# A hybrid decoder layer on eight cores: the last supertile's residual kept on chip, its silu inputs parked in SBUF, and a new order of early loads and of GpSimd's turns

## The chip, the cores and the metric

The kernel runs on the 8 NeuronCores of one Trainium2 chip. Each core takes one of the 8 sequences of the batch and shares nothing with the others but the weights that it reads. The metric is the device time of the slowest core, in microseconds. A core has TensorE (PE, matrix products into PSUM), VectorE (DVE), ScalarE (ACT), GpSimd (POOL, which cannot read PSUM) and SyncE (SP, which here only issues DMAs). PSUM has 8 banks of 128 x 512 floats.

## The reference, cut to what matters

```python
h = rmsnorm(x, norm_g)                                  # x: (8, 4096, 1024)
q, k, v, z_a, u_s, v_s, z_s = split(h @ w_in + b_in)    # 512,128,128,512,512,512,512 columns
attn = banded_sink_attention(q, k, v, sinks) * silu(z_a)
sgu = gelu(u_s) * (W_s @ layernorm(gelu(v_s)) + b_s) * silu(z_s)
x = x + concat(attn, sgu) @ w_out + b_out
out = rmsnorm(x, final_norm_g)
```

Attention has 8 query heads of 64 over 2 key heads, a window of 128 keys, and is evaluated on blocks of 128 queries against their own and the previous block of keys. W_s is a lower-triangular 128 x 128 matrix per group of 64 channels, applied inside chunks of 128 positions.

## The kernel before, in words

A core's 4096 rows are 32 tiles of 128 rows, four to a supertile of 512 (NS = 8 supertiles, `st`). Weights are loaded once, scaled by the norm's gain and kept in bf16 (`w_fm`, `w_vs`, `w_v`, line 463); w_out comes in bf16 through eight DMAs on GpSimd's queue (`load_w_out`, line 777).

For a supertile, x is loaded into `xa` (line 429, four slots, one per tile), squared on ScalarE (468), its norm finished in two small GpSimd steps (474, 477), scaled into `xn` (482, 483) and transposed into `xT`: through PSUM for the first two supertiles, by a DMA transpose (493) later. `fm_group` (511 to 528) makes 128 output columns for 512 rows: eight matmuls of 128 x 128 by 512 (line 517) into a bank, and an eviction with the bias: on ScalarE or VectorE for q and k (523, 524), on ScalarE with gelu or silu for u, z_s, z_a (527). `qkv` also makes v (542, 546). `vs_tile` (571 to 589) makes v_s with its layer norm, `mix_part` (617 to 629) the spatial gating. `attention` (645 to 704) handles one block: scores (647), exponential (652), mask multiply (665 on VectorE, 660 on GpSimd), sum of the two halves (682), values and denominators (674, 677), log and exponential of the denominator (690, 694), gate (696), and the product into `mixT` (701).

The output of a tile: `load_xe` loads the same rows of x again, as the residual, into one of four slots of `xe` (709), and GpSimd adds b_out to it (711). `out_tile` does two halves of eight matmuls (725), each evicted by VectorE into xe (730), a square on ScalarE (733), two GpSimd steps (735, 737), a scaling on VectorE by the norm and gain (739), and the store (742). A slot of xe is loaded again once its store has landed. The four loads of the last supertile are issued from the end of `build_program`'s loop (816 to 818).

The order of the work is not written by hand. `Graph.op` records every operation with what it reads and writes, a planned cost in us, and a priority (lower goes first); `Scheduler.run` then plays the program through with these costs and gives each engine a fixed order, always taking the operation that can start earliest. Three of its rules matter here. ScalarE works in phases, because each of its functions needs its own table: gelu, silu and exp of a supertile follow each other, with a table load between (line 424 in the trace), and matmul groups for gelu and silu have a gate: they are not planned before their phase, or the end of the one before it. PSUM banks have classes with a cap each (line 111): S for scores, pairs of banks; V for values and denominators, two per block; P for everything else. And operations marked `port=True` on VectorE and GpSimd are planned so as not to overlap (lines 141 to 143, 222). On the chip only semaphores hold: `emit` (268) gives each operation waits for its `deps`, and planned times that don't come true are not kept. Each engine, and each queue of DMA issues on SP, works strictly in its order.

```python
            if o.port and e in ("dve", "pool"):
                port[0] = free[e]
```

## Time and profile before

| what | value |
|---|---|
| median of 3 runs | 534.2 us (534.0 to 534.81) |
| the profiled execution, its own time | 536.34 us |
| its span, slowest core (core 0) | 534.8 us |
| spans of the eight cores | 528.0 to 534.8 us |
| TensorE busy | 483.6 us |
| VectorE busy | 379.2 us |
| ScalarE busy | 325.6 us |
| GpSimd busy | 191.6 us |

The profile is one execution on the slowest core; its times run from the first instruction. Busy times count instructions at work, not waits. An instruction that is held up inside, by a shared resource, shows as a long one. In a window or page row, the clock is the share of TensorE's full clock that was granted.

### The profile page before, as it was taken

How to read it: one execution, taken by the hardware profiler on the slowest of the kernel's cores; microseconds unless marked ns; L12 is line 12 of the kernel's file. 1: busy time of each engine (PE TensorE's matmuls, PEld its weight loads, DVE VectorE, ACT ScalarE, POOL GpSimd, SP SyncE). 2: the span in 40 equal slices, each digit the busy share in tenths (PEclk: the TensorE clock that was granted, in tenths of full speed). 3: DMA queues.
4: the chain of work that ended last, by engine and by line, in shares of the span. 5: the costliest groups of instructions: out<-in, count | busy, mean ns of one | idle time of the engine just before them, and what ended most of it. 6: DMA issues, size and time to landing. Idle time of an engine off the chain costs nothing.

```text
span 534.8 us, 9042 instructions; the slowest of 8 cores (528.0 to 534.8 us)
## 1 busy us (share of the span) xinstructions
PE 483.6 (90%) x2802; PEld 221.5 (41%) x2852; DVE 379.2 (71%) x527; ACT 325.6 (61%) x565; POOL 191.6 (36%) x232
## 2 busy tenths in 40 slices
PE   1799986898999999999999999999999999999960
PEld 0357442344444434444444434443444435443320
DVE  1676889659778767778775597766757687557963
ACT  4363393855677475847675756858578575348621
POOL 1030564125023331333236254542364215450444
PEclk9999997999999999999999999999999999999985
DMA  7999993593008801336532933356342213300363
GB/s 233 329 344 324 313 232 50 106 253 116 1 40 203 230 1 40 120 66 172 159 104 59 210 101 119 119 94 146 126 152 65 51 63 136 119 1 39 120 182 132
DMA packets 44543, 73.12 MB, mean 137 GB/s; under 512 B 27600, under 2 KB 27728, under 8 KB 44496
## 3 DMA queue, kind: packets, MB, share of 16 engines
q1 hardware_dynamic: 43200, 70.40, 44.5%
q0 software_dynamic: 1152, 2.10, 2.4%
q8 instruction: 23, 0.38, 0.3%
q14 instruction: 24, 0.20, 0.1%
q10 hardware_dynamic: 144, 0.05, 0.1%
HBM read 51.56 MB, written 16.78 MB: 128 GB/s over the span
## 4 chain that ended last, share of the span: by engine, by line
PE 79%; issue 5%; DVE 4%; ACT 4%; POOL 3%; DMA 3%; SPq 0%; POOLq 0%; DVEq 0%; ACTq 0%
PE pp L517 40%; PE pp L725 18%; PE pp L571 9%; PE pp L674 3%; PE pp L647 3%; PE pp L542 2%; DMA xa<-x 2%; PE pp L556 1%; DMA xe<-x 1%; PE pp L677 1%; PE pp L617 1%; DVE PT L665 1%; DVE xe L739 1%; POOL w_out_bf L777 1%; ACT PT L652 1%
## 5 line engine op out<-in xcount | busy, mean ns | idle before, releaser
L517 PE MATMUL pp<-xT,w_fm 128*128 128x512 bf16 x1056 | 243.0, 382 | 6.9 <-DVE sgt L625 1.6
L517 PEld LDWEIGHTS pp<-xT,w_fm 128*128 128x128 bf16 x1088 | 104.2, 98 | 134.8 <-issue 15.9
L725 PE MATMUL pp<-w_out_bf,mixT 128*128 128x512 bf16 x497 | 117.8, 384 | 6.2 <-DVE mixT L701 3.8
L711 POOL TENSOR_TENSOR xe<-xe,bout_sb 128x1024 f32<-128x1024 f32 x32 | 77.4, 2423 | 29.7 <-DMA xe<-x 29.6
L725 PEld LDWEIGHTS pp<-w_out_bf,mixT 128*128 128x128 bf16 x512 | 47.9, 99 | 69.1 <-issue 18.0
L733 ACT ACTIVATE junk<-xe 128x1024 bf16<-128x1024 f32 x32 | 34.0, 1062 | 53.8 <-DVE xe L730 48.5
L730 DVE TENSOR_TENSOR xe<-pp,xe 128x512 f32<-128x512 f32 x64 | 43.4, 685 | 28.9 <-PE pp L725 24.1
L652 ACT ACTIVATE PT<-pp 128x1024 bf16<-128x1024 f32 x63 | 62.6, 1030 | 0.9 <-PE pp L647 0.9
L571 PE MATMUL pp<-w_vs,xT 128*128 128x512 bf16 x221 | 53.7, 391 | 6.6 <-DVE v_r L546 5.3
L739 DVE SCALAR_TENSOR_TENSOR xe<-xe,st_fr,gf_sb 128x1024 f32<-128x1024 f32 x32 | 47.1, 1473 | 15.4 <-POOL st_fr L737 9.5
L665 DVE TENSOR_TENSOR PT<-PT,pack_b_sb 128x1024 bf16<-128x1024 bf16 x57 | 50.4, 898 | 4.8 <-ACT PT L652 4.0
L690 ACT ACTIVATE LR<-pp,esink 128x128 f32<-128x128 f32 x128 | 36.3, 365 | 26.7 <-PE pp L677 26.0
L578 ACT ACTIVATE vs_f<-vs_f 128x512 f32<-128x512 f32 x32 | 19.6, 627 | 42.0 <-DVE vs_f L576 40.5
L735 POOL TENSOR_SCALAR st_fm<-st_fs 128x1 f32<-128x1 f32 x32 | 9.9, 309 | 95.9 <-ACT junk L733 95.4
L527 ACT ACTIVATE zaT<-pp,pack_a_sb 128x512 bf16<-128x512 f32 x32 | 21.7, 691 | 33.5 <-PE pp L517 32.2
L576 DVE TENSOR_TENSOR vs_f<-pp,bvs_sb 128x512 f32<-128x512 f32 x32 | 22.0, 688 | 26.1 <-PE pp L571 21.9
L468 ACT ACTIVATE junk<-xa 128x1024 bf16<-128x1024 f32 x32 | 33.7, 1055 | 6.0 <-DMA xa<-x 5.2
L571 PEld LDWEIGHTS pp<-w_vs,xT 128*128 128x128 bf16 x224 | 21.8, 100 | 35.5 <-issue 11.9
L629 POOL TENSOR_TENSOR mixT<-sgt,uT 128x512 bf16<-128x512 f32 x19 | 22.0, 1156 | 40.6 <-DVE sgt L625 33.8
L625 DVE SCALAR_TENSOR_TENSOR sgt<-pp,pack_b_sb,Cmat 128x512 f32<-128x512 f32 x32 | 23.2, 745 | 16.5 <-PE pp L617 8.9
L584 POOL TENSOR_SCALAR st_ve<-st_mv 128x1 f32<-128x1 f32 x32 | 8.5, 266 | 71.0 <-DVE st_mv L582 70.1
L424 ACT ACT_TABLE_LOAD x24 | 30.8, 1283 | 1.9 <-POOL ones L439 1.5
(63 smaller groups left out, 542.6 us busy)
## 6 DMA issues: line engine op xcount, KB each, us to landing
xa<-x SPq DMA_DIRECT2D x32, 512.0 KB, 8.4
xe<-x SPq DMA_DIRECT2D x32, 512.0 KB, 4.1
out<-xe SPq DMA_DIRECT2D x32, 512.0 KB, 2.9
xe<-w_in SPq DMA_DIRECT2D x12, 512.0 KB, 12.1
mixT<-w_in SPq DMA_DIRECT2D x10, 512.0 KB, 14.3
w_out_bf<-w_out POOLq DMA_DIRECT2D x8, 256.0 KB, 15.7
LR<-sgu_wT SPq DMA_DIRECT2D x1, 512.0 KB, 11.4
bout_sb<-bout_bc SPq DMA_DIRECT2D x1, 512.0 KB, 13.1
```

The source lines that it names most:

```text
L424: return lambda e: e.activation(out=dmy[:, 1:2], in_=dmy[:, 0:1], func=func)
L468: G.op("act", lambda e: e.activation(out=junk[:], in_=xa[:, tt, :], func=AF.Square, accum_out=st_ss[:, par, tt:tt + 1]), reads=[("xa", tt) ...
L517: ins = e.matmul(bank(h), lhsT=w_fm[:, FM.index(cb), k, :], rhs=xT[:, xb, k, :], start=(k == 0), stop=(k == 7))
L571: ins = e.matmul(bank(h), lhsT=xT[:, xb, k, tt * 128:(tt + 1) * 128], rhs=w_vs[:, k, :], start=(k == 0), stop=(k == 7))
L652: G.op("act", lambda e, h=h, kb=kb: e.activation(out=PT[:, p2, kb, :], in_=bank2(h), func=AF.Exp, scale=0.125), uses=[h], writes=[("PT", p ...
L665: return e.tensor_tensor(out=v, in0=v, in1=mask[kb].unsqueeze(1).to_broadcast([128, 8, 128]), op=ALU.mult)
L690: ins = e.activation(out=LR[:, lb, c * 128:(c + 1) * 128], in_=bank(hd)[:, c * 128:(c + 1) * 128], func=AF.Ln, bias=esink[:, c:c + 1])
L711: G.op("pool", lambda e: e.tensor_tensor(out=xe[:, s, :], in0=xe[:, s, :], in1=bout[:], op=ALU.add), reads=["c_bout"], writes=[("xe", s, 0 ...
L725: ins = e.matmul(bank(h), lhsT=mixT[:, mb, ec, tt * 128:(tt + 1) * 128], rhs=w_out[:, ec, hf * 512:(hf + 1) * 512], start=(ec == 0), stop= ...
L730: G.op("dve", lambda e, hf=hf, h=h: e.tensor_tensor(out=xe[:, s, hf * 512:(hf + 1) * 512], in0=bank(h), in1=xe[:, s, hf * 512:(hf + 1) * 5 ...
L733: G.op("act", lambda e: e.activation(out=junk[:], in_=xe[:, s, :], func=AF.Square, accum_out=st_fs[:, s:s + 1]), reads=[("xe", s, 0), ("xe ...
L739: G.op("dve", lambda e: e.scalar_tensor_tensor(out=xe[:, s, :], in0=xe[:, s, :], scalar=st_fr[:, s:s + 1], in1=gf[:], op0=ALU.mult, op1=AL ...
```

## The change

There are five parts. (1) The last supertile's output uses `xa`, which still holds its x, in place of xe: `load_xe` is not called for it, b_out is added to xa by GpSimd, and the result is stored from xa; for the others nothing is changed but that the addition now stands in `out_tile`. (2) The last supertile's eight silu matmul groups have no gate; their result plus bias is copied to SBUF in fp32, by VectorE or ScalarE, into the other buffer of xT (z_s) and the weights of q (z_a), after the last readers of these; ScalarE applies silu from there in the silu phase. (3) The loads of the third supertile's x, of the first supertile's residual and of the final gain wait until the last part of w_out has landed, and w_out's operations are recorded earlier. (4) A GpSimd operation marked for the port waits for the VectorE operation marked for it that the plan has just before; line 739 is marked too. The other way round there is no wait. (5) Class V may hold three banks. Beside these, matmuls that write column ranges of one bank set the start flag only on the bank's first matmul; `full` and `onto` of a bank are new and `onto` is used by no caller. The diff, cut to its core:

```diff
...
+        for r in behind:
+            deps[id(r)] = r
...
-    CAPS = {"S": 4, "V": 2, "P": 4}
+    CAPS = {"S": 4, "V": 3, "P": 4}
...
-        port = [0.0]
+        port = [0.0, None]
...
             if o.port and e in ("dve", "pool"):
-                port[0] = free[e]
+                if e == "pool" and port[1] is not None and port[1].eng == "dve" and port[1] not in o.deps:
+                    o.deps.append(port[1])
+                port[:] = [free[e], o]
...
         def load_xa(st, tt):
             after = [w_op[X1_AFTER[tt] - 1]] if st == 1 else [w_op[NCB - 1]] if st == 2 else ()
             o = G.op("sp", lambda e: e.dma_start(out=xa[:, tt, :], in_=x_d[(4 * st + tt) * 128:(4 * st + tt + 1) * 128, :]),
-                 writes=[("xa", tt)], cost=0.5, dsem=d_xa[tt], kb=512, prio=st - 1.5 + 0.01 * tt, after=after)
+                 reads=[("w_out", 7)] if st == 2 else [], writes=[("xa", tt)], cost=0.5, dsem=d_xa[tt], kb=512, prio=st - 1.5 + 0.01 * tt, after=after)
...
-            G.op("pe", mm, reads=[("xT", xb, t) for t in range(4)] + [("w", cb)], cost=1.73, alloc=[h], prio=prio, mode="full", gate=ph)
+            pre = st == NS - 1 and func == AF.Silu
+            G.op("pe", mm, reads=[("xT", xb, t) for t in range(4)] + [("w", cb)], cost=1.73, alloc=[h], prio=prio, mode="full",
+                 gate=None if pre else ph)
...
+            if pre:
+
+                i = cb - CB_ZS
+                if i < 4:
+                    mem, old = xT[:, 1 - xb, 2 * i:2 * i + 2, :].rearrange("p a b -> p (a b)"), [("xT", 1 - xb, t) for t in range(4)]
+                else:
+                    mem, old = w_fm[:, i - 4, :, :].rearrange("p a b -> p (a b)"), [("w", CB_Q + i - 4)]
+                mem = mem.bitcast(F32)
+                G.op({"dve": (0.745, lambda e: e.tensor_scalar(out=mem, in0=bank(h), scalar1=bias, scalar2=None, op0=ALU.add)),
+                      "act": (0.69, lambda e: e.activation(out=mem, in_=bank(h), func=AF.Identity, bias=bias))},
+                     None, uses=[h], reads=["c_biasfm"], writes=[("pre", i)], prio=prio, behind=[r for k in old for r in G.rd[k]])
+                G.op("act", lambda e: e.activation(out=dst, in_=mem, func=func), reads=[("pre", i)], writes=[key], cost=0.6,
+                     prio=prio - 0.3, phase=ph)
+            elif func is None:
...
-                                       rhs=w_v[:, k, :], start=(k == 0), stop=(k == 7))
+                                       rhs=w_v[:, k, :], start=(k == 0 and tt == 0), stop=(k == 7),
+                                       skip_group_check=True)
...
-            G.op("sp", lambda e: e.dma_start(out=xe[:, s, :], in_=x_d[n * 128:(n + 1) * 128, :]), writes=[("xe", s, 0), ("xe", s, 1)],
+            G.op("sp", lambda e: e.dma_start(out=xe[:, s, :], in_=x_d[n * 128:(n + 1) * 128, :]), writes=[("xe", s), ("xe", s, 0), ("xe", s, 1)],
+                 reads=[("w_out", 7)] if st == 0 else [],
                  cost=0.5, dsem=d_xe[s], kb=512, prio=st + 0.2 + 0.1 * s)
-            G.op("pool", lambda e: e.tensor_tensor(out=xe[:, s, :], in0=xe[:, s, :], in1=bout[:], op=ALU.add),
-                 reads=["c_bout"], writes=[("xe", s, 0), ("xe", s, 1)], cost=2.6, prio=st + 0.6 + 0.1 * s, port=True)
...
+            last = st == NS - 1
+
+            buf, key = (xa, ("xa", s)) if last else (xe, ("xe", s))
+            G.op("pool", lambda e: e.tensor_tensor(out=buf[:, s, :], in0=buf[:, s, :], in1=bout[:], op=ALU.add),
+                 reads=["c_bout"], writes=[key], cost=2.4, prio=st + 0.6 + 0.1 * s, port=True)
...
-                def mmo(e, hf=hf, h=h):
+                cols = slice(hf * 512, (hf + 1) * 512)
+                need = [("mixA", mb, tt)] + [("mixS", mb, jj) for jj in range(4)] + [("w_out", k) for k in range(8)]
+                def mmo(e, cols=cols, h=h):
...
-                G.op("pe", mmo, reads=[("mixA", mb, tt)] + [("mixS", mb, jj) for jj in range(4)] + [("w_out", k) for k in range(8)],
-                     cost=1.73, alloc=[h], prio=v0 + 0.05 * hf, mode="full")
-                G.op("dve", lambda e, hf=hf, h=h: e.tensor_tensor(out=xe[:, s, hf * 512:(hf + 1) * 512], in0=bank(h),
-                                                                  in1=xe[:, s, hf * 512:(hf + 1) * 512], op=ALU.add),
-                     uses=[h], writes=[("xe", s, hf)], cost=0.68, prio=v0 - 0.5)
...
+                G.op("pe", mmo, reads=need, writes=[("oT", h)], cost=1.73, alloc=[h], prio=v0 + 0.05 * hf, mode="full")
+                G.op("dve", lambda e, cols=cols, h=h: e.tensor_tensor(out=buf[:, s, cols], in0=bank(h), in1=buf[:, s, cols], op=ALU.add),
+                     uses=[h], reads=[("oT", h), key], writes=[key + (hf,)], cost=0.68, prio=v0 - 0.5)
+            both = [key + (0,), key + (1,)]
...
-            G.op("dve", lambda e: e.scalar_tensor_tensor(out=xe[:, s, :], in0=xe[:, s, :], scalar=st_fr[:, s:s + 1], in1=gf[:],
+            G.op("dve", lambda e: e.scalar_tensor_tensor(out=buf[:, s, :], in0=buf[:, s, :], scalar=st_fr[:, s:s + 1], in1=gf[:],
                                                          op0=ALU.mult, op1=ALU.mult),
-                 reads=[("fr", s), "c_gf"], writes=[("xe", s, 0), ("xe", s, 1)], cost=1.39, prio=v0)
-            G.op("sp", lambda e: e.dma_start(out=out_d[n * 128:(n + 1) * 128, :], in_=xe[:, s, :]),
-                 reads=[("xe", s, 0), ("xe", s, 1)], cost=0.5, dsem=d_xe[s], kb=512, prio=v0, final=True)
+                 reads=[("fr", s), "c_gf"], writes=both, cost=1.3, prio=v0, port=True)
+            G.op("sp", lambda e: e.dma_start(out=out_d[n * 128:(n + 1) * 128, :], in_=buf[:, s, :]),
+                 reads=both, writes=[key], cost=0.5, dsem=d_xa[s] if last else d_xe[s], kb=512, prio=v0, final=True)
...
             load_const("c_bout", bout[:], bout_d, eng="sp", kb=512, prio=-0.3, after=[w_op[21]])
-            load_const("c_gf", gf[:], gf_d, eng="sp", kb=512, prio=-0.3, after=[w_op[21]])
+            load_const("c_gf", gf[:], gf_d, eng="sp", kb=512, prio=-0.3, after=[w_op[21]], reads=[("w_out", 7)])
...
         for cb in range(NCB):
             load_w(cb)
+        load_w_out()
...
         setup_late()
-        load_w_out()
...
         for tt in range(4):
-            load_xe(4 * (NS - 1) + tt)
             out_tile(4 * (NS - 1) + tt)
...
```

## Rows read from the trace of the kernel before

**Rows 1.** The page, busy us of each engine, share of the span, instructions.

```profile
PE 483.6 (90%) x2802; PEld 221.5 (41%) x2852; DVE 379.2 (71%) x527; ACT 325.6 (61%) x565; POOL 191.6 (36%) x232
```

**Rows 2.** Windows: length; busy PE, PEld, DVE, ACT, POOL (count); clock; DMA; GB/s.

```profile
60.00:64.00 4.00, 3.95 (x25) 1.79 (x24) 3.35 (x7) 0.00 (x0) 3.85 (x5) 1.00 1.02 335
...
70.00:108.00 38.00, 29.46 (x186) 12.85 (x188) 31.92 (x39) 25.09 (x47) 15.21 (x11) 0.91 0.62 124
108.00:478.00 370.00, 363.31 (x2055) 163.57 (x2093) 265.88 (x389) 241.80 (x422) 137.35 (x159) 1.00 0.39 110
478.00:502.00 24.00, 23.79 (x117) 9.16 (x117) 18.50 (x25) 17.30 (x29) 6.29 (x8) 1.00 0.18 67
502.00:520.00 18.00, 13.93 (x60) 5.44 (x60) 14.21 (x15) 6.66 (x16) 8.31 (x11) 0.91 0.48 141
520.00:534.80 14.80, 0.00 (x0) 0.00 (x0) 5.64 (x7) 2.30 (x4) 6.15 (x6) 0.57 0.37 148
```

**Rows 3.** Timeline, 70 to 108 us: start, us, engine, line, instructions merged.

```profile
74.29 10.63 POOL L711 TENSOR_TENSOR xe<-xe,bout_sb 128x1024 f32<-128x1024 f32 x4
...
75.83 9.64 DVE L665 TENSOR_TENSOR PT<-PT,pack_b_sb 128x1024 bf16<-128x1024 bf16 x4
...
87.42 5.84 PE L571 MATMUL pp<-w_vs,xT 128*128 128x512 bf16 x16 [5.26 <-DVE v_r L546]
...
93.96 3.63 PE L725 MATMUL pp<-w_out_bf,mixT 128*128 128x512 bf16 x16
```

**Rows 4.** Lines 665 and 739, whole span: ns min/median/max, first and last start.

```profile
L665 DVE TENSOR_TENSOR PT<-PT,pack_b_sb x57: 678/684/2842, 75.8 to 500.0; 128x1024 bf16<-128x1024 bf16 x57
...
L739 DVE SCALAR_TENSOR_TENSOR xe<-xe,st_fr,gf_sb x32: 1269/1284/3165, 104.7 to 530.4; 128x1024 f32<-128x1024 f32 x32
```

**Rows 5.** Timeline, 510 us to the end.

```profile
511.01 3.16 DVE L739 SCALAR_TENSOR_TENSOR xe<-xe,st_fr,gf_sb 128x1024 f32<-128x1024 f32 x1 [0.45 <-POOL st_fr L737]
511.03 8.81 PE L725 MATMUL pp<-w_out_bf,mixT 128*128 128x512 bf16 x31 [3.01 <-DVE mixT L701]
...
514.70 1.21 SPq L709 DMA_DIRECT2D xe<-x  x2
...
521.56 4.64 POOL L711 TENSOR_TENSOR xe<-xe,bout_sb 128x1024 f32<-128x1024 f32 x2 [2.59 <-DMA xe<-x]
...
526.37 1.29 DVE L730 TENSOR_TENSOR xe<-pp,xe 128x512 f32<-128x512 f32 x2 [1.02 <-POOL xe L711]
```

**Rows 6.** Waits: engine, line, waited for: us in total, times, longest.

```profile
DVE xe L739 <- POOL st_fr L737: 9.5, 9, 2.6
...
DVE xe L730 <- POOL xe L711: 4.6, 2, 3.6
...
PE pp L674 <- DVE mixT L701: 1.4, 1, 1.4
```

**Rows 7.** Timeline of SP: DMA issues from 46 to 103 us.

```profile
46.86 4.29 SPq L429 DMA_DIRECT2D xa<-x  x4
52.06 4.93 SPq L709 DMA_DIRECT2D xe<-x  x4
98.77 4.30 SPq L493 DMA_TRANSPOSE xT<-xn  x3
```

**Rows 8.** The tile w_out_bf: its DMA issues, and us from issue to landing.

```profile
L777 POOL DMA_DIRECT2D w_out_bf<-w_out x8: 535/557/760, 60.1 to 67.5; - x8
...
DMA to landing us min/median/max: 9.0/15.7/18.2
```

**Rows 9.** The page, DMA queue 0: packets, MB, share of 16 engines.

```profile
q0 software_dynamic: 1152, 2.10, 2.4%
```

**Rows 10.** Groups by line: busy us, mean ns, idle before.

```profile
L424 ACT ACT_TABLE_LOAD x24 | 30.8, 1283 | 1.9 <-POOL ones L439 1.5
...
L578 ACT ACTIVATE vs_f<-vs_f 128x512 f32<-128x512 f32 x32 | 19.6, 627 | 42.0 <-DVE vs_f L576 40.5 <-DVE st_mv L582 1.5
...
L524 ACT ACTIVATE qT<-pp,pack_a_sb 128x512 bf16<-128x512 f32 x17 | 11.6, 692 | 17.4 <-PE pp L517 17.3
```

More of the change, by code:

```diff
@@ L44, with __init__ @@
 class Bank:
-    def __init__(self, cls, size=1):
-        self.cls, self.size = cls, size
+    def __init__(self, cls, size=1, full=True, onto=False):
+        self.cls, self.size, self.full, self.onto = cls, size, full, onto
         self.at = None
@@ L70, in op @@
     def op(self, eng, fn, reads=(), writes=(), cost=0.1, prio=0.0, alloc=(), uses=(), phase=None, gate=None, mode=None,
-           dsem=None, kb=0, final=False, after=(), port=False):
+           dsem=None, kb=0, final=False, after=(), port=False, behind=()):
         o = Op()
@@ L164, in pick_banks @@
                     if any(bank_owner[c] is not None or c in taken for c in cells):
+                        continue
+                    if b.onto and not all(bank_full[c] for c in cells):
                         continue
@@ L236, in run @@
                         bank_owner[c] = b
+                        bank_full[c] = b.full
                         for u in bank_last[c]:
@@ L415, in build_program, with load_const @@
         d_once = []
-        def load_const(key, dst, src, eng="act", kb=64, prio=0.0, after=()):
+        def load_const(key, dst, src, eng="act", kb=64, prio=0.0, after=(), reads=()):
             s = sem(f"d_c{len(d_once)}")
             d_once.append(s)
-            G.op(eng, lambda e: e.dma_start(out=dst, in_=src), writes=[key] if isinstance(key, str) else key, cost=0.5,
+            G.op(eng, lambda e: e.dma_start(out=dst, in_=src), reads=reads, writes=[key] if isinstance(key, str) else key, cost=0.5,
                  dsem=s, kb=kb, prio=prio, after=after)
@@ L495, in transpose_x @@
                 return
-            h = Bank("P")
+            h = Bank("P", full=False)
             def tr(e):
@@ L724, in mmo @@
                     for ec in range(8):
[L725 removed]
+                        ins = e.matmul(bank(h), lhsT=mixT[:, mb, ec, tt * 128:(tt + 1) * 128], rhs=w_out[:, ec, cols],
                                        start=(ec == 0), stop=(ec == 7))
                     return ins
[L728 to L729 removed]
@@ L735, in out_tile @@
+                G.op("dve", lambda e, cols=cols, h=h: e.tensor_tensor(out=buf[:, s, cols], in0=bank(h), in1=buf[:, s, cols], op=ALU.add),
+                     uses=[h], reads=[("oT", h), key], writes=[key + (hf,)], cost=0.68, prio=v0 - 0.5)
+            both = [key + (0,), key + (1,)]
+            G.op("act", lambda e: e.activation(out=junk[:], in_=buf[:, s, :], func=AF.Square, accum_out=st_fs[:, s:s + 1]),
+                 reads=both, writes=["junk", ("fs", s)], cost=1.25, prio=v0)
             G.op("pool", lambda e: e.tensor_scalar(out=st_fm[:, s:s + 1], in0=st_fs[:, s:s + 1], scalar1=1.0 / D, scalar2=EPS,
```

15 lines of the change are left out of this document (7 added, 8 removed).

## The prediction

> **What bounds the kernel now.** I read the busy shares first, then the idle time of TensorE stretch by stretch, then what ended it in the two stretches where it is large. TensorE is busy for 483.6 of 534.8 us, VectorE for 379.2 [rows 1], so the question is where TensorE's 51 us of idle time lie. By stretch [rows 2]: of 370 us between 108 and 478 it is idle for 6.7 (370 - 363.31), of 24 until 502 for 0.2, but of 38 us between 70 and 108 for 8.5 (38 - 29.46), between 502 and 520 for 4.1 (18 - 13.93), and after 520 it does nothing for 14.8. The remaining 16.9 us, before 70, are the start, where inputs and weights arrive. The middle is TensorE's. An edit is worth something at 70 to 108, in which the first supertile's attention runs, or at the end.
>
> At 70 to 108, one wait stands out [rows 3]. GpSimd adds b_out to four residual tiles without a break (10.63 us), and four of VectorE's mask multiplies (line 665) lie beside them for 9.64 us. A mask multiply alone takes 0.68 us, at worst 2.84, which is about one GpSimd add [rows 3, 4]: VectorE stands still until the add is over. TensorE then waits 5.26 us for v_r, queued behind these multiplies, and the 16 matmuls after that take 5.84 us where 16 of the same size take 3.63 soon after [rows 3]: the granted clock is 0.91 of full over the stretch [rows 2], TensorE having been idle, and these run near the lower level, 1.2 instead of 2.4 GHz.
>
> At the end, the last two residual tiles are requested at 514.70, because their slots in xe must first be scaled (3.16 us on VectorE beside a GpSimd add, 1.28 as a rule) and stored [rows 4, 5]. Their b_out additions start at 521.56, when TensorE has finished (511.03 + 8.81 = 519.84). The tail therefore waits for a load, though the same rows of x were read for the norm.
>
> **The change part by part.** Durations are of the profiled execution: span 534.8 us, its own time 536.34, so 1.5 lie around the span; the median of the runs is 534.2, 2.1 below that time. I work out what the span loses and take it from the median.
>
> *Residual kept in xa.* Four loads and their issues go; four b_out additions of 2.3 us (4.64 for two, [rows 5]) stay, but can run as soon as xa is scaled, long before the end. The tail becomes: TensorE ends, the last eviction, square, two small GpSimd steps, scaling, store. TensorE's work from 502 on is 13.93 us [rows 2]. Its last 31 recorded matmuls (32 issued) took 8.81 us [rows 5]; at 3.63 us per 16 [rows 3] they would take 7.3, so 1.5 are slow clock and 12.4 are work: TensorE could end at 514.4 instead of 519.8. From the last eviction's start (526.37 plus half of 1.29) to the span's end are 7.8 us [rows 5], and with 0.2 allowed for the semaphore ahead of it 8.0. The best end is 522.4, a gain of 12.4. But the fourth attention block's chain still ends in an output tile that nothing can hide entirely: of the 4.1 us idle I keep 2.1, and take **10.3**. The lower end is 2.7, see the third rival. VectorE, the next in line, is busy for 18.50 + 14.21 + 5.64 us from 478 on [rows 2], partly in blocked instructions, so it could be done before 520 and isn't the bound.
>
> *GpSimd waits its turn.* Every GpSimd instruction marked for the port now waits for the VectorE one that the planner put before it. What it removes at 70 to 108: the excess of the four multiplies, 9.64 - 4 x 0.68 = 6.9 us of VectorE, seen by TensorE as 5.26 us of wait and 5.84 - 3.63 = 2.2 us of slow clock. I take **7.5**. Above, the whole stretch could give 8.5 + 2.2 = 10.7; below, 0, if the stall moves to another place. Queued behind a waiting add on GpSimd are the small steps of the norms (lines 584, 587, 735, 737), and behind those VectorE's scalings; VectorE already waits 9.5 us for st_fr in all [rows 6]. Over the middle VectorE is busy 265.88 of 370 us [rows 2], so even a doubled wait is covered: cost 0, and at worst what the fifth rival says. Marking line 739 as a port user falls under the same sum.
>
> *w_out ahead of residual loads.* Now the third supertile's x (four loads issued from 46.86), the first residuals (four from 52.06) and gf go ahead of w_out on the DMA engines, and w_out's eight transfers land up to 18.2 us after issue, the last issued at 67.5 [rows 7, 8]. In the changed kernel these nine loads wait in SP's queue for w_out; behind them on SP are only the transposes of the third supertile, at 98.77 now [rows 7]. w_out takes 2.4% of the span on all engines, 12.8 us [rows 9]; issued from 60.1 [rows 8], it should have landed at about 76. The nine loads, 4.7 MB at 335 GB/s, the rate of 60 to 64 us [rows 2], take another 14, until 91 or so with landing. The first output projections run at 94 [rows 3], and GpSimd's additions get later, which by itself moves them away from these multiplies. Gain and cost 0; cover lost, the price is the second rival's.
>
> *Silu inputs of the last supertile.* The eight matmul groups lose their gate, so they can fill idle slots in earlier phases; TensorE's work is the same. Added: eight evictions of 0.69 us [rows 10], 5.5 us; the silu itself now reads SBUF, 0.63 instead of 0.69 [rows 10]. ScalarE is idle for a third of the middle and VectorE for over a quarter [rows 2], so this is hidden. What may not be: the silu phase becomes a ScalarE-only stretch of two table loads of 1.28 and 8 x 0.63 us, 7.6 us in all [rows 10], under which TensorE can only run output projections that were filler for the last attention. Value 0; ends: a gain of 2, if the attention starts earlier, and a loss of 7.6.
>
> *Third V bank.* One wait of line 674 for line 701, 1.4 us [rows 6], goes; up to 6.7 us of middle idle could [rows 2]. Below, a third V bank takes a bank from the projections: a loss of the same size. I take **1.0**, nearest the row. The start flags of matmuls add no instruction.
>
> Sum: 10.3 + 7.5 + 1.0 = 18.8 us. The span becomes 516.0, the median 534.2 - 18.8 = **515.4 us**.
>
> **The rivals.**
> *The stall is not removed.* Only GpSimd waits; a multiply that comes late still meets an add under way and loses up to 2.16 us (2.84 - 0.68). For it: the planner of before kept the two apart on paper as well. Against: the four adds run without a break now, which a wait for the multiply between them forbids. Without the 7.5: 522.9 us.
> *w_out lands late.* It is issued while VectorE is busy for 3.35 us of the 4 from 60 to 64 [rows 2], and nine loads now stand behind it. If it lands at about 85 as now (67.5 + 18.2), the residuals land from 87 to 100, and the wait for them replaces the stall: the 7.5 are gone, 522.9 us. Against: these landing times come from a queue with 4.7 MB of other loads ahead. The Trainium skill ("SBUF — State Buffer", the box on the DVE blocks DMA trap) says that a DMA issued from GpSimd's queue cannot get its descriptors written while VectorE holds the port pair; it speaks for this rival, and by it the sum would be 11.3 us instead of 18.8. The trace here shows late landing, but not whether port or queue causes it.
> *The end turns to ScalarE.* The 7.6 us stretch uses up TensorE's filler, the last attention then leaves TensorE idle that long, and the tail gains 10.3 - 7.6 = 2.7: 523.0 us. For it: the last supertile has no next one to fill with. Against: with these projections as filler TensorE was idle for only 0.2 us between 478 and 502 [rows 2], so that there is some room.
> *Nothing in sum.* The first or second of these with the third leaves 2.7 + 1.0 = 3.7 us, and bank waits of that size end at 534.2.
> *Slower.* One mechanism: the turn-taking makes the b_out additions late. Each of 32 waits for a VectorE instruction, the eviction (line 730) waits for the addition, its bank is held, and TensorE stands. It decides from 18.8 / 32 = 0.6 us per addition that reach TensorE. With the whole 1.28 us of a scaling instruction [rows 4] in two of three additions (0.85 each), 27 us: 534.2 - 18.8 + 27 = 542.4 us. Against: TensorE is idle for only 6.7 us in the middle, and VectorE waited for an addition only twice, 4.6 us in all [rows 6].
>
> **How the numbers follow.** Forecast 0.62; stall not removed 0.10; w_out late 0.08; ScalarE at the end 0.12; nothing in sum 0.02; slower 0.06. The likeliest case gives 515.4. Its best is 12.4 + 10.7 + 2 = 25.1 less than 534.2, about 509. The three middle cases end at 523; with 1.5 for bank waits the range ends at 524.5. It leaves out 0.08 and the edges of the forecast. A measurement of this kernel tells about 0.2%, 1 us. Faster 0.92, the same 0.02, slower 0.06.
>
> **What would show it.** Right: no load into xe after the seventh supertile's; no line 665 row of 2.8 us in an unbroken series near 80, and v_r not waited for; matmuls at full clock between 80 and 95; last store about 8 us after TensorE's last matmul, and TensorE's end near 508 in a span near 516. Silu evictions beside earlier phases, middle idle still about 6 us. Wrong: GpSimd additions still in a block across multiplies; the first residual landing after 87 with line 730 waiting for it; TensorE idle for over 5 us in the last attention; TensorE waiting for line 730 throughout.

## The result and the profile after

The changed kernel takes 518.06 us (median of four runs, 517.63 to 519.86) against 534.5 us of the kernel before on the same chip, a ratio of 0.970 [0.967, 0.973]. The forecast was 515.4; the gain of 16.4 us is 2.4 less than the 18.8 of the sum. The sign and the size are about right, but the runs below give the parts other prices than the prediction did. Several chips were used, so each run is given as a ratio to the kernel before on its own chip; 0.001 is 0.53 us. On the last of these chips one half ran at a lower granted clock in most runs, so for three kernels only cores 4 to 7, the undisturbed half, are compared with the same cores of the kernel before.

The page of the changed kernel, slowest core (own time 518.4, span 516.8), with busy time by engine and the group of VectorE's mask multiply:

```profile
PE 486.8 (94%) x2852; PEld 220.7 (43%) x2852; DVE 355.9 (69%) x524; ACT 339.6 (66%) x576; POOL 180.7 (35%) x232
...
L694 DVE TENSOR_TENSOR PT<-PT,pack_b_sb 128x1024 bf16<-128x1024 bf16 x58 | 42.9, 760 | 1.8 <-ACT PT L681 1.5
```

The mask multiplies take 42.9 us for 58, where 58 of 0.68 are 39.4. Before it was 50.4 for 57, on the page of that kernel, so 8 of some 12 us of standing still are gone; the longest single one still takes 2.83 us, about as in [rows 4]. By stretch, in the columns of [rows 2]:

```profile
70.00:108.00 38.00, 34.16 (x206) 14.60 (x205) 25.67 (x39) 24.89 (x48) 15.99 (x13) 0.91 0.63 163
108.00:478.00 370.00, 369.78 (x2109) 164.02 (x2106) 255.42 (x389) 260.50 (x439) 141.34 (x164) 1.00 0.40 114
478.00:502.00 24.00, 24.00 (x123) 9.34 (x122) 21.75 (x33) 18.15 (x37) 2.62 (x6) 1.00 0.11 44
502.00:520.00 18.00, 6.02 (x28) 2.55 (x26) 9.73 (x11) 4.24 (x8) 3.71 (x10) 0.82 0.43 175
```

TensorE's idle time between 70 and 108 fell from 8.5 us to 3.8 on this core, still at a mean clock of 0.91 (on all eight, from 6.4 to 8.5 us to 1.1 to 4.1). After 502 it works for 6 us instead of 13.9. In the middle it fell from 6.7 us to 0.2, but most of that is no gain. The trace of before on this core has 2802 matmuls [rows 1], the changed one 2852: 50 records are missing, 32 of line 517, 15 of line 725, 3 of line 571. Core 1 of before, which has no gaps, shows:

```profile
108.00:478.00 370.00, 368.30 (x2101) 164.28 (x2100) 264.21 (x390) 242.80 (x425) 138.44 (x160) 1.00 0.39 112
```

The middle had 1.7 us to give there, and 1.7 to 3.6 on the six cores without gaps, not 6.7.

The timeline of the changed kernel at 70 to 108 us (start, duration, engine, line; line 694 is 665 of before, 751 is 711, 759 is 725, 763 is 730, 730 is 701, 725 is 696):

```profile
77.16 1.94 DVE L694 TENSOR_TENSOR PT<-PT,pack_b_sb 128x1024 bf16<-128x1024 bf16 x3
...
79.38 3.63 PE L599 MATMUL pp<-w_vs,xT 128*128 128x512 bf16 x16
...
87.28 4.65 POOL L751 TENSOR_TENSOR xe<-xe,bout_sb 128x1024 f32<-128x1024 f32 x2 [9.93 <-DMA xe<-x]
...
89.80 0.69 DVE L763 TENSOR_TENSOR xe<-pp,xe 128x512 f32<-128x512 f32 x1 [3.39 <-POOL xe L751]
...
90.41 2.07 DVE L725 TENSOR_TENSOR LR<-LR,zaT 128x512 f32<-128x512 f32 x1
...
93.83 9.84 PE L759 MATMUL pp<-w_out_bf,mixT 128*128 128x512 bf16 x32 [3.46 <-DVE mixT L730]
```

The multiplies now take 0.65 us each and nothing waits for v_r; the 16 matmuls at 79.38 run at full clock in 3.63 us. But another stall has come, 8 us later. The first residual landed at 87.28, after GpSimd had waited 9.93 us for it. Line 763 waited 3.39 us for the addition and held VectorE's queue, in which lines 725 and 730 stand behind it; line 725 then met the second addition and took 2.07 us instead of 0.68. TensorE waited 3.46 us for line 730, and then needed 9.84 us for 32 matmuls (mean granted clock 0.71), which take 7.26 at the 3.63 per 16 above. So this core still pays 6 us here.

The other cores of the same execution show what decides. On core 1 the residual was there earlier:

```profile
81.31 4.68 POOL L751 TENSOR_TENSOR xe<-xe,bout_sb 128x1024 f32<-128x1024 f32 x2 [6.46 <-DVE mixT L658]
...
88.60 7.07 PE L759 MATMUL pp<-w_out_bf,mixT 128*128 128x512 bf16 x32 [0.73 <-DVE mixT L730]
```

On cores 1, 2, 4 and 6 the first addition starts between 81.3 and 82.7 us, and TensorE waits 0.73 us at this place; on cores 0, 3, 5 and 7 it starts between 85.1 and 87.3, after waiting for its load, and TensorE waits 2.3 to 3.5 us. The first four span 508.9 to 511.9 us, the others 513.8 to 516.8, and the time is that of the slowest.

The end of core 0:

```profile
499.66 8.37 PE L759 MATMUL pp<-w_out_bf,mixT 128*128 128x512 bf16 x38
...
508.81 2.47 DVE L772 SCALAR_TENSOR_TENSOR xa<-xa,st_fr,gf_sb 128x1024 f32<-128x1024 f32 x2
...
511.44 0.19 POOL L768 TENSOR_SCALAR st_fm<-st_fs 128x1 f32<-128x1 f32 x1 [2.10 <-DVE xa L772]
...
512.57 1.28 DVE L772 SCALAR_TENSOR_TENSOR xa<-xa,st_fr,gf_sb 128x1024 f32<-128x1024 f32 x1 [1.29 <-POOL st_fr L770]
```

TensorE ends at 508.0 (499.66 + 8.37), the span at 516.8: the tail is 8.8 us, and 8.8 to 9.0 on every core, where it was 12.7 to 15.0.

### The profile page after: what moved, and what is told of

It is laid out like the page before. It is cut to its first block, busy times and chain, and to the rows that moved or that the text cites. A ratio compares the mean times of both kernels' runs of the same rounds, so it can differ in the third digit from the quotient of the medians.

```text
span 515.2 us, 9245 instructions; the slowest of 8 cores (508.9 to 516.8 us)
## 1 busy us (share of the span) xinstructions
PE 485.8 (94%) x2852; PEld 220.6 (43%) x2852; DVE 355.7 (69%) x524; ACT 339.2 (66%) x576; POOL 180.8 (35%) x232
## 4 chain that ended last, share of the span: by engine, by line
PE 87%; DMA 3%; DVE 3%; ACT 2%; issue 2%; POOL 2%; POOLq 0%; SPq 0%; DVEq 0%; ACTq 0%
PE pp L528 45%; PE pp L759 21%; PE pp L599 8%; PE pp L703 3%; PE pp L676 3%; PE pp L568 2%; DMA xa<-x 2%; PE pp L645 1%; PE pp L583 1%; DMA xe<-x 1%; PE pp L706 1%; DVE xa L772 1%; DVE PT L694 1%; ACT junk L479 0%; ACT PT L681 0%
## 5 line engine op out<-in xcount | busy, mean ns | idle before, releaser
L528 PE MATMUL pp<-xT,w_fm 128*128 128x512 bf16 x1088 | 248.0, 382 | 2.8 <-ACT xT L519 1.3
L751 POOL TENSOR_TENSOR xe<-xe,bout_sb 128x1024 f32<-128x1024 f32 x28 | 66.2, 2372 | 30.8 <-DMA xe<-x 8.8
L759 PEld LDWEIGHTS pp<-w_out_bf,mixT 128*128 128x128 bf16 x512 | 47.8, 98 | 68.2 <-issue 16.7
L763 DVE TENSOR_TENSOR xe<-pp,xe 128x512 f32<-128x512 f32 x56 | 38.4, 686 | 20.4 <-PE pp L759 18.1
L772 DVE SCALAR_TENSOR_TENSOR xe<-xe,st_fr,gf_sb 128x1024 f32<-128x1024 f32 x28 | 37.6, 1343 | 19.5 <-POOL st_fr L770 18.3
L599 PE MATMUL pp<-w_vs,xT 128*128 128x512 bf16 x224 | 51.0, 379 | 0.0
L719 ACT ACTIVATE LR<-pp,esink 128x128 f32<-128x128 f32 x128 | 36.5, 368 | 17.1 <-PE pp L706 13.5
L694 DVE TENSOR_TENSOR PT<-PT,pack_b_sb 128x1024 bf16<-128x1024 bf16 x58 | 43.1, 763 | 1.7 <-ACT PT L681 1.5
L768 POOL TENSOR_SCALAR st_fm<-st_fs 128x1 f32<-128x1 f32 x32 | 7.5, 234 | 86.6 <-ACT junk L766 27.2
L766 ACT ACTIVATE junk<-xe 128x1024 bf16<-128x1024 f32 x28 | 29.5, 1054 | 12.4 <-DVE xe L763 11.1
L553 ACT ACTIVATE zaT<-pp,pack_a_sb 128x512 bf16<-128x512 f32 x28 | 18.8, 693 | 25.4 <-PE pp L528 25.4
L654 DVE SCALAR_TENSOR_TENSOR sgt<-pp,pack_b_sb,Cmat 128x512 f32<-128x512 f32 x32 | 23.3, 748 | 13.9 <-POOL mixT L658 8.1
L612 POOL TENSOR_SCALAR st_ve<-st_mv 128x1 f32<-128x1 f32 x32 | 6.1, 190 | 69.8 <-DVE st_mv L610 44.5
```

The lines of the kernel that those rows point to most:

```text
L528: ins = e.matmul(bank(h), lhsT=w_fm[:, FM.index(cb), k, :], rhs=xT[:, xb, k, :], start=(k == 0), stop=(k == 7))
L599: ins = e.matmul(bank(h), lhsT=xT[:, xb, k, tt * 128:(tt + 1) * 128], rhs=w_vs[:, k, :], start=(k == 0), stop=(k == 7))
L694: return e.tensor_tensor(out=v, in0=v, in1=mask[kb].unsqueeze(1).to_broadcast([128, 8, 128]), op=ALU.mult)
L719: ins = e.activation(out=LR[:, lb, c * 128:(c + 1) * 128], in_=bank(hd)[:, c * 128:(c + 1) * 128], func=AF.Ln, bias=esink[:, c:c + 1])
L751: G.op("pool", lambda e: e.tensor_tensor(out=buf[:, s, :], in0=buf[:, s, :], in1=bout[:], op=ALU.add), reads=["c_bout"], writes=[key], cos ...
L759: ins = e.matmul(bank(h), lhsT=mixT[:, mb, ec, tt * 128:(tt + 1) * 128], rhs=w_out[:, ec, cols], start=(ec == 0), stop=(ec == 7))
```

## Experiments

**Undo the kept residual.** The last supertile's residual is loaded into xe a second time; all else is the changed kernel.

```diff
-            last = st == NS - 1
+            last = False
...
+            load_xe(4 * (NS - 1) + tt)
             out_tile(4 * (NS - 1) + tt)
```

> The changed kernel, but the last supertile's residual is loaded into xe again. Theory (the reload bounds the end): the end waits for loads behind the stores, the stretch from TensorE's last matmul to the end goes from 8.8 us back to about 15, and TensorE loses some of the 4 us idle in the last attention: 524 to 529 us against 518. Rival (the end is earlier because the silu inputs were made early): under 2 us, 518 to 520.

Measured: 528.87 us, ratio 0.984 [0.981, 0.988], 7.6 us more than the changed kernel. The tail is 18.6 to 18.9 us on every core. Core 1, timeline of the end:

```profile
507.69 1.53 SPq L738 DMA_DIRECT2D xe<-x  x2
...
514.31 4.64 POOL L751 TENSOR_TENSOR xe<-xe,bout_sb 128x1024 f32<-128x1024 f32 x2 [1.67 <-DVE xe L772]
...
519.13 1.29 DVE L763 TENSOR_TENSOR xe<-pp,xe 128x512 f32<-128x512 f32 x2 [1.02 <-POOL xe L751]
```

TensorE ended at 509.0. The loads go out from 507.69, the last additions start 6.6 us later, and the last evictions wait for them. That the reload makes the tail long is shown, as the prediction had it. The size belongs to this kernel: before, with the same reload, the tail was 12.7 to 15.0 us, and here the last 1.67 us before the additions are a wait not for the load but, by the turn, for a scaling of VectorE.

**Only the kept residual,** in the kernel before.

```diff
+            last = st == NS - 1
+            buf, key = (xa, ("xa", s)) if last else (xe, ("xe", s))
...
-            load_xe(4 * (NS - 1) + tt)
             out_tile(4 * (NS - 1) + tt)
```

> The kernel before, with nothing of the change but the last supertile's residual kept in xa (its second load is gone; the planner works with its old costs otherwise). Theory (the step of the prediction): 10.3 us less, 523.9 us, a ratio of 0.978 to 0.983, and each core's span ends 8 to 9 us after TensorE's last matmul. Rival: what was taken from the changed kernel by undoing this step, 0.0143 of the time, is what it is worth, 0.984 to 0.988, because the last tiles then end TensorE's work earlier or later by a different order.

Measured: 536.99 us, ratio 0.996 [0.994, 0.999], a gain of only 2.0 us. Both expectations failed, though the tail is 8.4 to 8.5 us on every core, where it was 12.7 to 15.0. Something gives the time back earlier. Core 1, timeline:

```profile
413.66 7.48 POOL L721 TENSOR_TENSOR xa<-xa,bout_sb 128x1024 f32<-128x1024 f32 x3
413.85 5.07 DVE L589 TENSOR_SCALAR vln<-vs_f,st_mv,st_lr 128x512 bf16<-128x512 f32 x2
...
419.18 1.08 PE L617 MATMUL pp<-WT_bf,vln 128*64 128x128 bf16 x32 [1.38 <-DVE vln L589]
...
430.28 2.79 POOL L721 TENSOR_TENSOR xa<-xa,bout_sb 128x1024 f32<-128x1024 f32 x1
...
430.79 2.82 DVE L682 TENSOR_TENSOR PC<-PT 128x1024 bf16<-128x1024 bf16 x1
...
433.86 0.63 PE L674 MATMUL pp<-PT,v_r 128*64 128x512 bf16 x4 [2.38 <-DVE PC L682]
```

With no second load, the additions of the last supertile are ready as soon as xa has been scaled. GpSimd takes three in a row (7.48 us), in the seventh supertile's work. VectorE's line 589 beside them takes 5.07 us for two; a single one takes 0.55 where nothing overlaps it. TensorE waited 1.38 us for vln. The fourth addition comes alone, at 430.28, and costs more: line 682 beside it takes 2.82 us instead of 0.67, and TensorE waits 2.38 us for it. So it needs no block of additions to hold TensorE, only one that meets a VectorE instruction for which TensorE is waiting. Both waits stand on all eight cores (1.4 and 2.4 us). Before, the stretch from 400 to 440 held 40 us of TensorE's work on this core, here 36.

**Only GpSimd's turn,** in the kernel before.

```diff
+                if e == "pool" and port[1] is not None and port[1].eng == "dve" and port[1] not in o.deps:
+                    o.deps.append(port[1])
-                port[0] = free[e]
+                port[:] = [free[e], o]
```

> The kernel before, with nothing of the change but GpSimd's wait for its turn, in the same order of work. Theory (the step of the prediction): the stretched multiplies near 80 us come back to about 0.7 us each, V is waited for no more, and the time falls by 5 to 8 us, to a ratio of 0.985 to 0.991. Rival C: the additions go behind the multiplies but the residual loads and w_out still collide, so only the stall moves: ratio 0.994 to 1.002. Rival D: waiting in turn slows it, 1.006 or more.

Measured: 529.75 us, ratio 0.985 [0.981, 0.989], 8.2 us. Core 1, timeline:

```profile
75.37 2.35 POOL L713 TENSOR_TENSOR xe<-xe,bout_sb 128x1024 f32<-128x1024 f32 x1
...
76.91 3.17 DVE L667 TENSOR_TENSOR PT<-PT,pack_b_sb 128x1024 bf16<-128x1024 bf16 x4
...
81.43 2.36 POOL L713 TENSOR_TENSOR xe<-xe,bout_sb 128x1024 f32<-128x1024 f32 x1 [3.70 <-DVE mixT L631]
...
83.17 3.63 PE L573 MATMUL pp<-w_vs,xT 128*128 128x512 bf16 x16
```

The additions that ran as one block of 10.63 us [rows 3] now stand apart, at 75.37, 81.43 and later; four multiplies take 3.17 us instead of 9.64, and no wait for v_r follows. The step stands as predicted, by the rows and by the time, which is a little better than the range of the theory. The tail is still 13.5 us or more.

**Undo the turn** in the changed kernel.

```diff
-                if e == "pool" and port[1] is not None and port[1].eng == "dve" and port[1] not in o.deps:
-                    o.deps.append(port[1])
```

> The changed kernel in the same order on every engine, but GpSimd's added waits for VectorE's port instructions are taken out. Theory (the waits removed the stall near 80): multiplies of 2.8 us come back and TensorE idles again, 523 to 526 us. Rival (the residuals now land after 85, and that alone parts additions and multiplies): within 2 us of 518, perhaps 1 us less, since the last norm step on GpSimd waits 1.1 us for a scaling at the end.

Measured: 524.95 us, ratio 0.976 [0.972, 0.980], 3.3 us slower than the changed kernel, less than the theory had and more than the rival. The rival's reason holds near 80 us: the multiplies stay at 0.68 us, since the residuals land after them. The loss is where the kept residual hurt alone. Core 1:

```profile
408.32 7.32 POOL L749 TENSOR_TENSOR xa<-xa,bout_sb 128x1024 f32<-128x1024 f32 x3
...
410.87 2.56 DVE L615 TENSOR_SCALAR vln<-vs_f,st_mv,st_lr 128x512 bf16<-128x512 f32 x1
...
413.69 1.92 PE L643 MATMUL pp<-WT_bf,vln 128*64 128x128 bf16 x32 [2.38 <-DVE vln L615]
```

Again three additions of xa in a row, stretched VectorE work (0.55 alone, 2.56 here), and TensorE waiting 2.38 us, on every core.

**Both together,** in the kernel before, to test whether the turn guards what the kept residual opens: the edits of the two runs with one part alone, the main lines of which are

```diff
+            buf, key = (xa, ("xa", s)) if last else (xe, ("xe", s))
...
+                    o.deps.append(port[1])
```

> The kernel before, with two parts of the change: the last supertile's residual kept in xa, and GpSimd's wait for its turn. Alone they gave 0.9963 and 0.9846. Theory A: the first makes the last supertile's additions ready early, they ran three in a row from 413.7 us and held VectorE and then TensorE; with the turn they are parted, and the whole of the tail's 5.2 us (13.6 to 8.4) comes through: 0.970 to 0.977, less than the 0.981 that the two give if they merely add up, and no line-589 instruction over 1.5 us between 405 and 425 us. Theory B: they add up, 0.979 to 0.984.

Measured: 522.82 us, ratio 0.970 [0.968, 0.971]. Theory A, at the edge of its range. The two alone would add up to 0.981; together they reach the ratio of the whole change. Core 1:

```profile
410.03 2.37 POOL L723 TENSOR_TENSOR xa<-xa,bout_sb 128x1024 f32<-128x1024 f32 x1 [1.13 <-DVE uT L625]
...
410.75 1.08 PE L619 MATMUL pp<-WT_bf,vln 128*64 128x128 bf16 x32
...
413.43 2.35 POOL L723 TENSOR_TENSOR xa<-xa,bout_sb 128x1024 f32<-128x1024 f32 x1 [1.04 <-DVE mixT L631]
```

The additions to xa are parted by VectorE's work, and TensorE waits for nothing there. Between 108 and 478 us it is idle for 0.7 us on each of the six cores without gaps, with the kept residual alone for 4.9 to 7.3.

**Undo the order behind w_out** (gf, the first residuals and the third supertile's x wait for nothing).

```diff
-                 reads=[("w_out", 7)] if st == 2 else [], writes=[("xa", tt)], cost=0.5, dsem=d_xa[tt], kb=512, prio=st - 1.5 + 0.01 * tt, after=after)
+                 writes=[("xa", tt)], cost=0.5, dsem=d_xa[tt], kb=512, prio=st - 1.5 + 0.01 * tt, after=after)
...
-                 reads=[("w_out", 7)] if st == 0 else [],
...
-            load_const("c_gf", gf[:], gf_d, eng="sp", kb=512, prio=-0.3, after=[w_op[21]], reads=[("w_out", 7)])
+            load_const("c_gf", gf[:], gf_d, eng="sp", kb=512, prio=-0.3, after=[w_op[21]])
```

> The changed kernel, but the loads of x of the third supertile, of the first residual and of the gain don't wait for w_out. Theory (the order costs: on core 0 ScalarE waits 4.05 us for x at 91.67, TensorE stands 3.5 us behind it and then runs 32 matmuls in 9.84 us): 512 to 515 us. Rival 1 (the prediction's: gain and cost nothing): 517 to 519. Rival 2 (w_out late holds up the first projections or the additions meet the multiplies again): 521 to 526.

Measured: 526.34 us, ratio 0.978 [0.974, 0.982], 4.3 us slower than the changed kernel. The wait for x alone therefore does not explain what is left. Core 1:

```profile
81.54 5.14 POOL L750 TENSOR_TENSOR xe<-xe,bout_sb 128x1024 f32<-128x1024 f32 x2 [3.71 <-DVE mixT L658]
...
84.38 2.84 DVE L694 TENSOR_TENSOR PT<-PT,pack_b_sb 128x1024 bf16<-128x1024 bf16 x1
...
93.88 3.57 PE L758 MATMUL pp<-w_out_bf,mixT 128*128 128x512 bf16 x8 [4.36 <-DVE mixT L730]
```

Early residuals make the additions ready while the attention needs VectorE: two of them run from 81.54, one multiply meets them and takes 2.84 us, and TensorE then stands 4.36 us at line 758 and runs 8 matmuls in 3.57 us, nearly twice the 1.90 at full clock. That multiply's excess is 2.2 us, so it is at most a part of the wait; VectorE works without a break from 81.9 to 93.8, and the rest is what else stands ahead of line 730 in its queue. The turn does not help the multiply: it holds GpSimd behind VectorE, not VectorE behind GpSimd.

**Free x alone** (gf and the residuals still wait): only the first of the three edits above.

> The changed kernel, with the third supertile's x no longer held back behind w_out (gf and the four residual loads still are). Theory A: what is left of the stall near 90 us is the wait for x, since the cores whose x landed late are those whose TensorE stood 2.3 to 3.5 us; then the time falls by 2 to 5 us, to a ratio of 0.961 to 0.967 against the kernel before, and the square of the third supertile's first tile waits under 3 us. Theory B: loads that overlap w_out cost as much as they give, as in the run where nothing waited for w_out (0.978): ratio 0.968 to 0.980.

Measured: 516.26 us, ratio 0.959 [0.955, 0.962]. Theory A by the direction, and more than its range: 6.1 us faster than the changed kernel, and the two intervals do not meet. Core 0, the window from 70 to 108 and rows of its timeline:

```profile
70.00:108.00 38.00, 37.30 (x232) 17.00 (x235) 28.36 (x49) 31.09 (x58) 16.32 (x16) 1.00 0.47 113
```

```profile
88.69 2.35 POOL L751 TENSOR_TENSOR xe<-xe,bout_sb 128x1024 f32<-128x1024 f32 x1
...
92.86 0.69 DVE L730 TENSOR_TENSOR mixT<-pp,LR 128x512 bf16<-128x512 f32 x1
...
93.47 1.28 DVE L763 TENSOR_TENSOR xe<-pp,xe 128x512 f32<-128x512 f32 x2
```

TensorE is idle for 0.7 us there instead of 3.8, at full clock (0.4 to 0.7 on all cores). The reason need not be the theory's. The first addition starts at 88.69, later than the 87.28 of the changed kernel, yet nothing waits: line 730 now stands ahead of line 763 in VectorE's queue, so the attention does not wait for a residual. How much of the 6.1 us comes from x being there and how much from this other order was not tried apart; the rows speak for the order.

**Only the order behind w_out,** in the kernel before.

```diff
+        load_w_out()
         for tt in range(4):
...
-        load_w_out()
...
+                 reads=[("w_out", 7)] if st == 0 else [], cost=0.5, dsem=d_xe[s], kb=512, prio=st + 0.2 + 0.1 * s)
```

x of the third supertile and gf get the same wait.

> The kernel before, with nothing of the change but w_out ahead of the residual loads, gf and the third supertile's x, which wait for it. Theory A: later residual loads put the additions behind the multiplies near 80 us, as the turn does, so the stall of 5.3 us and its slow stretch go by this means too: 0.984 to 0.990. Theory B (the step of the prediction, which counted this order at nothing): 0.996 to 1.003. Rival: the wait for the third supertile's x costs more than the stall it saves, over 1.003.

Measured: spans of 524.2 to 533.3 us on the four cores of the undisturbed half, where the kernel before has 528.1 to 533.4 in a run on this chip; its fastest run took 538.51 us, that of before 538.46. Theory B by the time, yet not by its reason. Core 6:

```profile
80.03 0.69 DVE L665 TENSOR_TENSOR PT<-PT,pack_b_sb 128x1024 bf16<-128x1024 bf16 x1 [0.27 <-ACT PT L652]
...
86.17 4.66 POOL L711 TENSOR_TENSOR xe<-xe,bout_sb 128x1024 f32<-128x1024 f32 x2 [9.96 <-DMA xe<-x]
...
89.30 2.07 DVE L665 TENSOR_TENSOR PT<-PT,pack_b_sb 128x1024 bf16<-128x1024 bf16 x1
...
93.32 5.30 PE L725 MATMUL pp<-w_out_bf,mixT 128*128 128x512 bf16 x16 [4.03 <-DVE mixT L701]
...
94.73 1.06 ACT L468 ACTIVATE junk<-xa 128x1024 bf16<-128x1024 f32 x1 [6.35 <-DMA xa<-x]
```

The multiplies near 80 us are short (0.69) and v_r is waited for no more, as theory A had it. In their place the additions come when the residual has landed, at 86.17, a multiply behind the first eviction meets the second of them (2.07), TensorE waits 4.03 us for line 701, and ScalarE 6.35 us for the third supertile's x. One stall was exchanged for another, the one that the changed kernel has on four of its cores.

**Hold the first additions, not the loads.** The version in which nothing waits for w_out, where each addition of the first supertile also waits until its tile's attention output is written.

```diff
-                 reads=["c_bout"], writes=[key], cost=2.4, prio=st + 0.6 + 0.1 * s, port=True)
+                 reads=["c_bout"] + ([("mixA", mb, tt)] if st == 0 else []), writes=[key], cost=2.4, prio=st + 0.6 + 0.1 * s, port=True)
```

> The run where nothing waited for w_out (0.978), but each bias addition of the first supertile also waits until that tile's attention output is written. Theory A: what cost time there was that early residuals make GpSimd's additions ready among the softmax multiplies, one of which took 2.84 us; without them there the stall of 4.4 us at line 758 near 90 us goes and the time comes to that of the run with only x freed, 0.956 to 0.966. Theory B: what cost time was the loads themselves running beside w_out: it stays at 0.974 to 0.982.

Measured: spans of 514.1 to 517.4 us on the undisturbed half; the kernel of the last experiment, which is the one with x freed but for small steps, has 510.7 to 512.6 there. The slowest of the four cores is at 0.968 of that of the kernel before (medians of 516.6 and 533.4 us), between the two theories. Core 6:

```profile
85.67 0.71 DVE L694 TENSOR_TENSOR PT<-PT,pack_b_sb 128x1024 bf16<-128x1024 bf16 x1
...
87.98 2.35 POOL L750 TENSOR_TENSOR xe<-xe,bout_sb 128x1024 f32<-128x1024 f32 x1 [2.15 <-DVE mixT L730]
...
88.50 2.38 DVE L725 TENSOR_TENSOR LR<-LR,zaT 128x512 f32<-128x512 f32 x1 [0.72 <-ACT LR L723]
...
92.01 1.27 DVE L762 TENSOR_TENSOR xe<-pp,xe 128x512 f32<-128x512 f32 x2
...
92.83 3.61 PE L758 MATMUL pp<-w_out_bf,mixT 128*128 128x512 bf16 x16 [2.45 <-DVE xe L762]
```

The stretched multiply and the stall of 4.4 us are gone (0.71; no wait for line 730). But the second addition, held until 87.98, meets another VectorE instruction: line 725 takes 2.38 us instead of 0.68, the eviction of line 762 stands behind it in the queue until 92.01, and line 758 waits 2.45 us for that. The row that theory A named went, its time did not come in full, and what the loads themselves cost stays open.

**Gate the last silu as before.**

```diff
-            pre = st == NS - 1 and func == AF.Silu
+            pre = False
```

> The changed kernel, but the last supertile's silu groups are gated and read PSUM as before. Theory (value nothing, the end is given by TensorE's work and the 8.8 us after it): 517 to 520 us. Rival (the early silu is what lets the last attention start 7 us earlier and keeps TensorE busy to the end): 521 to 525. Rival 2 (the ScalarE-only stretch costs): 514 to 516.

Measured: 519.94 us, ratio 0.968 [0.964, 0.972]: no difference that can be told.

**Two V banks** in the changed kernel.

```diff
-    CAPS = {"S": 4, "V": 3, "P": 4}
+    CAPS = {"S": 4, "V": 2, "P": 4}
```

> The changed kernel planned with two V banks as before. The prediction counted 1.0 us for the third bank: ratio 0.971 to 0.974. Rival: the idle time of TensorE between 108 and 478 us, which is under 1.5 us in the changed kernel, comes back with two banks: 3 to 6 us, 0.976 to 0.982. Rival: the third bank does nothing, 0.968 to 0.972.

Measured: 523.53 us, ratio 0.973 [0.969, 0.976], 1.3 us on paper; the interval takes in both the forecast of 1.0 and nothing. The rows are clearer than the time. Core 1:

```profile
510.13 5.15 PE L759 MATMUL pp<-w_out_bf,mixT 128*128 128x512 bf16 x16 [2.32 <-DVE mixT L730]
```

On every core TensorE waits 2.3 us for line 730 near the end, which it does on no core of the changed kernel, and the tail behind is 7.8 to 7.9 us, 1 us shorter. So the third bank takes away a wait at the end, not the one of line 674 from which the forecast had its 1.0.

**Turn for the additions only,** with x freed.

```diff
-                if e == "pool" and port[1] is not None and port[1].eng == "dve" and port[1] not in o.deps:
+                if e == "pool" and cost > 2 and port[1] is not None and port[1].eng == "dve" and port[1] not in o.deps:
```

> The run with only x freed (0.9585), where of GpSimd's instructions only the residual additions (planned at over 2 us) wait for their turn and the small ones do not. Theory: in the tail the last norm's small steps no longer wait 1.1 us for VectorE, so each core's span ends 7.6 to 8.0 us after TensorE's last matmul in place of 8.8 to 9.0; the rest is as it was: 0.954 to 0.960. Rival: small steps that run inside VectorE's instructions hold them up as additions do, 0.961 or more, with line-589 or line-694 instructions over 1.5 us.

Measured: spans of 510.7 to 512.6 us on the undisturbed half, with tails of 8.6 us. The theory failed by 0.6 us of tail, and by its time: the slowest of these cores is at 0.962 of that of the kernel before (medians of 513.3 and 533.4 us), where the rival begins. Core 4:

```profile
502.90 2.47 DVE L772 SCALAR_TENSOR_TENSOR xa<-xa,st_fr,gf_sb 128x1024 f32<-128x1024 f32 x2
...
504.49 0.93 POOL L768 TENSOR_SCALAR st_fm<-st_fs 128x1 f32<-128x1 f32 x1 [1.30 <-ACT junk L766]
```

The step after the square starts at once, but it takes 0.93 us beside VectorE's scaling, where in the changed kernel it took 0.19 (at 511.44) after waiting for its turn. In the tail the wait stands for time that the instruction would have spent nearly all anyway. In the middle TensorE is idle for 2.6 us on each of cores 5 to 7, against 0.8 to 1.5 on the cores without gaps in the run with x freed. Whether the small steps that run without a turn cause that, as the rival has it, is not shown: instructions of lines 617 and 694 over 1.5 us stand in both traces.

## Why the prediction came out near, and where it was wrong

**Kept residual, 10.3 us: mis-sized, and not on its own.** The tail fell by 5.2 us (13.6 to 8.4, the middle of the cores) in the run with this part alone and its end is as described; the 8.0 us of the forecast were 8.8 in the changed kernel. The step that failed is that "TensorE could end at 514.4": the idle time between 502 and 520 was to come back as an earlier end, while the additions "can run as soon as xa is scaled, long before the end". That was counted as free. In the run alone it was the cost: the four additions between 413 and 433 us hold VectorE and take 4 us of TensorE's time, and 2.0 us of gain remain. A smaller error stands beside it: the sum read the tail from core 0, where it was 15.0 us, the longest of the eight. With the turn in place it is worth 8.1 us (0.9846 - 0.9695).

**Turn, 7.5 us: right alone, too small together.** Alone it gave 8.2 us, from the place that [rows 3] show. Added to the kept residual it gives 14.3 (0.9963 - 0.9695), since it also parts the additions that this brings into the middle. The two give 16.3 us (0.0305 of 534.2), the sum had 17.8 for them.

**Order behind w_out, 0 us: wrong in its parts.** The sentence "The first output projections run at 94" was the cover for loads that land until 91. With the stall gone the projections start at 86.31 in the changed kernel, so the cover went with the wait that made it. The second rival had this wait, and gave the wrong late-comer: w_out itself lands by 78.5 (68.2 + 10.3), the residuals from 87 on core 0. So one of the prediction's signs of being wrong, the first residual landing after 87 with the eviction waiting for it, came true on that core. The sum hides two effects: with the residuals and gf held and x freed, 0.959; with all held, 0.970; with none, 0.978. With the order of work that the planner makes in each case, holding x costs 6.1 us, and holding the residuals and gf saves 10.4.

**The rule of the Trainium skill** in that rival (the Trainium skill, "SBUF — State Buffer", the box on the DVE blocks DMA trap) does not show here. VectorE was busy for 7.27 of the ten us from 60 to 70 before, for 7.59 in the changed kernel, and for 7.90 on core 1 of the run where nothing waits for w_out. In the last two, w_out's transfers landed so:

```profile
DMA to landing us min/median/max: 4.8/8.7/10.3
```

```profile
DMA to landing us min/median/max: 9.1/15.7/18.3
```

The time follows the loads ahead of them: it is that of [rows 8] again when these return, with VectorE as busy in both. How long VectorE holds the pair no trace here tells, and its busy time need not be that time, so this speaks for the queue as the cause in this kernel and does not test the rule itself.

**Pre-loaded silu, 0 us:** as forecast, within what the runs tell. **Third V bank, 1.0 us:** by the time not told apart from nothing; by the rows it removes a wait of 2.3 us at the end, not the one it was priced by. The "6.7 us of middle idle" behind its upper end were mostly missing records.

**The other rivals.** "Slower" didn't come: in the changed kernel TensorE waits for line 763 for at most 0.3 us at a time on any core. ScalarE didn't become the bound: TensorE is busy for all 24 us from 478 to 502. "The stall is not removed" is half what happened: it went near 80, and a smaller one stands at 90.

**Luck in the total.** Taking w_out's order or the V bank out of the changed kernel costs 0.008 and 0.003, yet kept residual and turn alone reach the time of the whole change. So the sum left out a gain of some 4 us, of w_out's order, and a loss of some 5 that the parts make together. These nearly cancel, and that the total lies 2.4 us from the forecast is in part luck.

**What stays open.** Part of that loss is in the traces. By the middle of its eight cores the changed kernel spans 512.9 us against 531.8 before, 0.964, and kept residual with turn 518.5 against 533.3 on its chip, 0.972; it is without the two waits for the attention's last product near 500 us that the latter has on every core (0.8 to 1.1 and 1.95 us). But four of its cores pay for the late residuals near 90, and the slowest core is the time. The planner orders all work anew for each kernel, so parts don't add; what its other edits (costs of 2.4 and 1.3, scaling marked as a port user, bank flags) do was not tried.

## What to carry to other kernels

When an edit makes work ready earlier, ask where a greedy planner or an eager engine will put it, and what it holds up there: here four additions moved from the tail into the middle and cost most of what the tail had saved, one of them all by itself, until a turn kept them off the VectorE work that TensorE waits for. When a stall is to go, redo the timing of all that was hidden behind it, since what comes after moves up by as much. A load that is held back helps only if nothing waits for it first; hold each load alone before holding them together, and look at what then stands ahead of it in each queue.

## What was not expected of the hardware

Instructions of VectorE and GpSimd that overlap slow each other, on both sides. VectorE's mask multiply took 0.68 us alone and 2.84 beside an addition; GpSimd's 128x1 step took 0.19 us alone and 0.93 beside VectorE's scaling, so waiting in turn costs such a step hardly anything (tails of 8.6 us without, 8.8 to 9.0 with). The shortest 128x1024 addition took 2.34 to 2.35 us in every run.

A trace can lack 50 matmul records of one core, and its idle time then looks larger by 5 us in a stretch (6.7 us on core 0 of before, 1.7 on core 1); the count of weight loads on the same core (2852 beside 2802 in [rows 1]) or of matmuls on another shows it.
